# Half of the gate products moved into attention, with the recurrence on VectorE and softmax sums from a block of ones

## What is computed

```python
xn = rms_norm(x, g_mix_norm)
z = xn @ w_in
c_q, c_kv, k_r, u, gate_a, gate_b = jnp.split(z, IN_SPLITS, axis=-1)
q = (rms_norm(c_q, g_q_a) @ w_q_b).reshape(b, t, N_HEADS, QK_DIM)
...
attn = chunk_causal_mla(q_nope, q_rope, k_nope, kr_all, v, q_pos, k_pos)
u_c, lru_buf_new = causal_dwconv(u, lru_buf, lru_conv_w, lru_conv_b)
rec, h_last = rg_lru(u_c, h0, w_rg, b_rg, w_ig, b_ig, lru_lambda)
mixed = jax.nn.sigmoid(gate_a) * attn + jax.nn.sigmoid(gate_b) * rec
x = x + mixed @ w_out
up = rms_norm(x, g_ffn_norm) @ w_up
up_c, ffn_buf_new = causal_dwconv(up, ffn_buf, ffn_conv_w, ffn_conv_b)
gate, val = jnp.split(up_c, 2, axis=-1)
x = x + (jax.nn.silu(gate) * val) @ w_down
```

## Time and profile before

| | |
|---|---|
| median of 3 runs | 945.11 us (944.52 to 946.34) |
| the profiled execution | 945.21 us, span 943.3 us |
| mean granted TensorE clock | 0.982 of full speed |
| TensorE matmul busy | 899.4 us (95%), 6689 instructions |
| VectorE busy | 604.8 us (64%), 1182 instructions |
| ScalarE busy | 347.5 us (37%) |
| GpSimd busy | 238.3 us (25%) |
| chain that ended last | TensorE 86%, VectorE 6%, issue 4% |

### The profile page before, as it was taken

How to read it: one execution, slowest core, us unless ns; L and a number is a source line. 1 busy time by engine, 2 the same in 40 slices (tenths; PEclk the granted TensorE clock), 3 DMA queues, 4 the chain that set the end, 5 groups by cost and what they waited for, 6 DMA issues and landing times.

```text
span 943.3 us, 18508 instructions
## 1 busy us (share of the span) xinstructions
PE 899.4 (95%) x6689; PEld 847.8 (90%) x6689; DVE 604.8 (64%) x1182; ACT 347.5 (37%) x619; POOL 238.3 (25%) x278
## 2 busy tenths in 40 slices
PE   5999999998799999998999999999999999999998
PEld 5899999987577887776799999999999999999998
DVE  4378634686789888897544488777778777322221
ACT  6331455364344444442423533333333332112111
POOL 4000233462333221331012233333333333201000
PEclk8999999999899999997999999999999999999999
DMA  8333323322000000010003232233332222233321
GB/s 256 79 84 76 97 78 82 77 73 46 15 7 10 14 14 14 20 27 1 1 23 90 67 110 78 81 88 89 89 89 82 78 85 84 84 97 104 98 70 36
DMA packets 114630, 63.55 MB, mean 67 GB/s; under 512 B 7836, under 2 KB 113054, under 8 KB 114588
## 3 DMA queue, kind: packets, MB, share of 16 engines
q1 hardware_dynamic: 112396, 59.17, 22.4%
q0 software_dynamic: 2192, 3.81, 1.8%
HBM read 59.85 MB, written 2.70 MB: 66 GB/s over the span
## 4 chain that ended last, share of the span: by engine, by line
PE 86%; DVE 6%; issue 4%; ACT 2%; POOL 1%; SPq 1%; DMA 0%; DVEq 0%; ACTq 0%; POOLq 0%
PE PS L1141 61%; PE PS L1354 4%; PE PS L1338 4%; PE PS L1319 3%; PE PS L1176 3%; PE PS L1265 2%; PE PS L1308 2%; PE PS L1214 2%; PE PS L1261 1%; PE PS L1362 1%; PE PS L1292 1%; PE PS L1283 1%; DVE small L1010 1%; DVE w_lo L773 0%; PE PS L1325 0%
## 5 line engine op out<-in xcount | busy, mean ns | idle before, releaser
L541 ACT ACTIVATE w_hi<-w_raw 128x1024 fp32r<-128x1024 f32 (+2 forms) x104 | 107.6, 1035 | 368.7 <-PE PS L1141 354.4
L773 DVE TENSOR_TENSOR w_lo<-w_raw,w_hi 128x1024 fp32r<-128x1024 f32 (+2 forms) x104 | 128.1, 1231 | 122.8 <-ACT w_hi L541 122.6
L1141 PE MATMUL PS<-x2h,w_hi 128*128 128x274 f32 x704 | 147.7, 291 | 1.1 <-DVE w_lo L773 1.1
L1141 PE MATMUL PS<-x2h,w_lo 128*128 128x274 f32 x704 | 146.9, 290 | 0.0
L1141 PE MATMUL PS<-x2l,w_hi 128*128 128x274 f32 x704 | 146.9, 290 | 0.0
L1141 PEld LDWEIGHTS PS<-x2h,w_hi 128*128 128x128 f32 x704 | 111.9, 189 | 1.4 <-issue 1.3
L1141 PEld LDWEIGHTS PS<-x2l,w_hi 128*128 128x128 f32 x704 | 112.0, 189 | 0.0
L1141 PEld LDWEIGHTS PS<-x2h,w_lo 128*128 128x128 f32 x704 | 111.4, 189 | 0.0
L1141 PE MATMUL PS<-xnh,w_hi 128*128 128x274 f32 x384 | 83.3, 299 | 4.4 <-DVE w_lo L773 2.3
L1141 PE MATMUL PS<-xnl,w_hi 128*128 128x274 f32 x384 | 81.7, 295 | 0.0
L1141 PE MATMUL PS<-xnh,w_lo 128*128 128x274 f32 x384 | 81.0, 293 | 0.0
(11 more groups left out here) (254 smaller groups left out, 1706.6 us busy)
## 6 DMA issues: line engine op xcount, KB each, us to landing
w_raw<-in_w_up_dram SPq DMA_DIRECT2D x44, 512.0 KB, 3.8
w_raw<-in_w_in_dram SPq DMA_DIRECT2D x24, 512.0 KB, 3.9
w_raw<-in_w_down_dram SPq DMA_DIRECT2D x16, 512.0 KB, 3.7
w_raw<-in_w_out_dram SPq DMA_DIRECT2D x8, 512.0 KB, 4.1
w_raw<-in_w_down_dram SPq DMA_DIRECT2D x8, 384.0 KB, 3.9
xnat<-in_x_prompt_dram SPq DMA_DIRECT2D x4, 512.0 KB, 5.0
w_raw<-in_w_in_dram SPq DMA_DIRECT2D x4, 416.0 KB, 4.7
wq<-in_w_q_b_dram SPq DMA_DIRECT2D x8, 192.0 KB, 2.5
```

The source lines that it names most:

```text
L541: nc.scalar.activation(hi[:, slot % 2, 0:n], raw[:, slot % 4, 0:n], ACT.Copy).then_inc(s_hi, 1)
L773: tt(lo[:, slot % 2, 0:n], raw[:, slot % 4, 0:n], hi[:, slot % 2, 0:n].bitcast(F32), ALU.subtract).then_inc(s_lo, 1)
L1141: last = mm(PS[:, 2 * rank + j, 0:HT], w[:, slot % 2, cols], x[:, k0 + k, j * HT:(j + 1) * HT], start=(k0 + k == 0 and first), stop=(k0 + ...
```

## The change

Only twelve items stand ahead of attention (`FIRST`: A0, B0, U0 to U7, A1, B1). The other twelve gate items are computed inside attention, in halves of 24 matmuls (`gate_half`, banks 0 and 1), two items in pairs 0 to 4 and one in pairs 5 and 6 (`fills`). The sigmoids of the two branch gates become (1 + tanh(x/2))/2. The recurrence runs among the first products: squares of `a` go from GpSimd to ScalarE, the two products a block from GpSimd to VectorE. The key and query squares go from GpSimd to ScalarE. `V` gets a block of ones, so that a value matmul with a stationary tile of 128 columns leaves the sum of exponentials in the other 64 partitions; `values` now write banks 3 and 5, scores rotate over banks 2 and 4, and the transposition is a plain one with `ident`. ScalarE copies the sums (`head_sums`), VectorE takes their reciprocals over 128x274, twice a pair, one pair later (`sums_inverse`), and GpSimd multiplies and adds (`mix`). The first two output items are begun with k up to 6 and finished after that. `Kn` and `Qn` lie on the same memory as `th0` and `uc0` of the LRU's first four blocks. The hand-written loops up to attention are unrolled.

```diff
+FIRST = [("A", 0), ("B", 0)] + [("U", n) for n in range(KD)] + [("A", 1), ("B", 1)]
...
+I_LAT, I_IN = 0, 4
+I_G = I_IN + NF
+I_OUT = I_G + 12
...
+    return ("BA"[item % 2], 2 + (item - I_G) // 2)
...
+    return [I_G + 2 * p, I_G + 2 * p + 1] if p < 5 else [I_G + 5 + p] if p < 7 else []
...
+        zone = place
+        Kn = fixed("Kn", [P, 2, NKT, 2, NOPE])
...
+        th0 = fixed("th0", [P, 4, T])
+        uc0 = fixed("uc0", [P, 4, T])
...
-                                         accum_out=sm[:, 0:1]).then_inc(s_e, 1)
+                    nc.scalar.activation(Pn[:, n % 3, 0:w], bank[:, 0:w], ACT.Exp, bias=sm[:, 2:3]).then_inc(s_e, 1)
...
+                act.wait_ge(s_pv, 9 * p + 4 * (h + 1))
+                if h == 0 and p:
+                    act.wait_ge(s_mix, p)
+                nc.scalar.activation(sums[rows(h), 0:SEQ], values_bank(h)[rows(1 - h), :], ACT.Copy).then_inc(s_sum, 1)
...
             act.wait_ge(s_rec, 4)
...
+            for u in range(6):
+                evacuate_kq(0, u, (0, 1, 2, 3, 0, 1)[u])
+            squares_keys(0)
+            lru_gates(7)
+            squares_queries(0)
...
+                a_n = U[:, n, LEAD:]
+                dve.wait_ge(s_bt, n + 1)
+                step.on(nc.vector.tensor_copy(a_n[:, S0 - 1:S0], zero[:, 0:1]))
+                link(nc.vector.tensor_copy(uc(n)[:, S0 - 1:S0], vec[:, V_H0 + n:V_H0 + n + 1]))
+                nc.vector.tensor_tensor_scan(a_n, a_n, uc(n), 0.0, ALU.mult, ALU.add).then_inc(s_rec, 1)
...
+            def lru_input(n):
+                dve.wait_ge(s_mult, n + 1)
+                dve.wait_ge(s_iu, n + 1)
+                tt(uc(n), th(n), uc(n), ALU.mult).then_inc(s_bt, 1)
...
+                dve.wait_ge(s_lrui, n + 1)
+                tt(uc(n), tmp[:, n % 2, :], uc(n), ALU.mult).then_inc(s_iu, 1)
...
-            def row_inverse(p, n):
-                dve.wait_ge(s_e, p * 9 + (n + 1))
-                sm = small[:, 4 + n % 3, :]
-                if n < 8:
-                    link(nc.vector.reciprocal(sm[:, 1:2], sm[:, 0:1]))
...
+            def gate_half(item, j):
+                kind, m = gate_of(item)
+                if j == 0:
+                    dve.wait_ge(s_gp, item - I_G + 1)
...
-                ts(dg[:, n % 3, :], ident[:, :], sm[:, 1:2], None, ALU.mult).then_inc(s_dg, 1)
...
+                cols = slice(j * HT, (j + 1) * HT)
+                tt(gate(kind, m)[:, cols], PS[:, j, 0:HT], rsT[:, cols], ALU.mult).then_inc(s_gf, 1)
...
+            def gated_values(p, h):
+                g_p = gate("A", p)[rows(h), 0:SEQ]
+                dve.wait_ge(s_gt, gate_count("A", p))
+                dve.wait_ge(s_pv, 9 * p + 4 * (h + 1))
+                stt(g_p, g_p, 1.0, values_bank(h)[rows(h), :], ALU.add, ALU.mult).then_inc(s_o, 1)
...
+            def sums_inverse(p, j):
+                cols = slice(j * HT, (j + 1) * HT)
+                dve.wait_ge(s_sum, 2 * p + 2)
+                dve.wait_ge(s_o, 3 * p + 3)
+                ins = nc.vector.reciprocal(sums[:, cols], sums[:, cols])
+                if j:
+                    ins.then_inc(s_ri, 1)
...
+                    if n == 3:
+                        if following:
+                            columns(p + 1, 0, 0)
+                            columns(p + 1, 1, 1)
+                        if p:
+                            sums_inverse(p - 1, 0)
+                        if following:
+                            gate_half(gate_items[0], 0)
+                    if n == 4:
+                        gated_values(p, 0)
+                        if p:
+                            sums_inverse(p - 1, 1)
+                        if 1 <= p <= 5:
+                            split_item(17 + 2 * p)
+                        if following:
+                            gate_half(gate_items[0], 1)
...
+                        lru_m2(q)
+                if g == 8:
+                    for q in range(2):
+                        lru_input(q)
+                        recurrence(q)
+            evacuate_first(9)
+            gated_input(5)
+            conv(7)
+            for q in range(2, 4):
+                lru_input(q)
+                recurrence(q)
+            split_item(I_IN + 11)
+            gated_input(6)
...
+            def gate_half(item, j):
+                pe.wait_ge(s_lo, item + 1)
+                for k in range(KD):
+                    cols = slice(k * P, (k + 1) * P)
+                    for w, x, first in ((hi, xnh, True), (hi, xnl, False), (lo, xnh, False)):
+                        last = mm(PS[:, j, 0:HT], w[:, item % 2, cols], x[:, k, j * HT:(j + 1) * HT],
+                                  start=(k == 0 and first), stop=(k == KD - 1 and w is lo))
+                last.then_inc(s_used if j else s_gp, 1)
...
-                    last = mm(bank[:, a * P:(a + 1) * P], Pn[:, n % 3, a * P:(a + 1) * P], dg[:, n % 3, :], start=True, stop=True)
+                    last = nc.tensor.transpose(bank[:, a * P:(a + 1) * P], Pn[:, n % 3, a * P:(a + 1) * P], ident[:, :])
...
-                        last = mm(PS[h * VD:(h + 1) * VD, 3, t * P:(t + 1) * P], V[:, par, a, h, :], PT[:, b, a * P:(a + 1) * P],
...
+                        last = mm(values_bank(h)[:, t * P:(t + 1) * P], V[:, par, a, h:h + 2, :].rearrange("p h n -> p (h n)"),
...
+                    if following and n == 3:
+                        for v in range(2):
+                            if kq:
+                                pe.wait_ge(s_kqf, 6 * (p + 2) + 5 + v)
+                            else:
+                                pe.wait_ge(s_vf, 3 * p + 2 + v)
+                            transpose_kq(p + 1, v, v)
+                        pe.wait_ge(s_trf, 5 * (p + 1) + 1)
+                        gate_half(first, 0)
+                    if following and n == 4:
+                        pe.wait_ge(s_trf, 5 * (p + 1) + 2)
+                        gate_half(first, 1)
+                    if following and n == 5:
+                        for v in (2, 3):
...
+                    keys_queries(0, 0, 0)
+                    keys_queries(0, 1, 1)
+                    pe.wait_ge(s_free, 10)
+                    keys_queries(0, 2, 2)
+                    keys_queries(0, 3, 3)
+                    for u in (4, 5):
+                        pe.wait_ge(s_kqf, u - 3)
+                        keys_queries(0, u, u - 4)
+                    lru(7)
...
+            def output_product(r, k0, nk):
...
+            for r in range(2):
+                if r:
+                    pe.wait_ge(s_e, 9 * NP_)
+                    pe.wait_ge(s_o, 3 * NP_ - 2)
+                    pe.wait_ge(s_sum, 2 * NP_ - 1)
+                pe.wait_ge(s_lo, I_OUT + r + 1)
+                output_product(r, 0, KD - 1)
+            for r in range(2):
+                output_product(r, KD - 1, 1).then_inc(s_used, 1)
+            for r in range(2, KD):
                 pe.wait_ge(s_free, G_OUT + r - 1)
```

More of the change, by code:

```diff
@@ L369, in _ @@
+            for t in range(I_OUT + 6, I_UP):
+                w_out_item(t)
             with sp.Fori(0, NU // 4) as it:
@@ L715, in _ @@
+            act.wait_ge(s_free, 12)
+            gate_tanh(gate("B", 1))
+            for u in range(4, 6):
+                evacuate_kq(1, u, u - 4)
+            squares_keys(1)
+            last_states(1)
+            for u in range(3):
+                evacuate_v(0, u, (0, 1, 5)[u])
+            exps(0, 0)
+            squares_queries(1)
+            for p in range(NP_):
+                attend(p)
+            mixed_hi(7)
             with act.Fori(0, 2) as it:
@@ L1396, in _ @@
[L1396 to L1410 removed]
+                        scores(p + 1, n - 7)
+                    transpose_probs(p, n)
```

1087 lines of the change are left out of this document (627 added, 460 removed).

## The result

The changed kernel takes 915.62 us (median of 4 runs, 914.76 to 915.99) against 944.82 us of the kernel before on the same chip: a ratio of 0.969, 95% interval 0.9674 to 0.9706. It is 29 us faster, where 18 were forecast. The profiled execution has a span of 914.2 us.

What follows compares the result with a forecast made beforehand. The prediction took TensorE as the bound, with VectorE second. Its terms, start -3.7, first products +5.8, attention -24.0 and output +3.5, sum to -18.4 us: 927 us from a median of 945.11, range 911 to 940.

Steps and rivals of the forecast that it cites:

- rival 2: Better packing: start chains side by side (-12), attention stalls 4 us, sample loads hidden (-7); 905 to 918 us, chance 0.22.
- The start: Up to the first product: a 2.09 us wait and 1.6 us of lower clock go, -3.7 us.
- (b): First products, up to the second pair of scores: waits and low clock grow from 21.6 to 27.4 us, +5.8 us.
- The first wait: First products: evacuation of pair 0's keys waits for recurrences 0 to 3 on VectorE, 7.3 us of TensorE wait.
- With 7 us of small waits: First products: small waits besides the two large ones, put at a third of what there was.
- the second place: Before attention goes on: VectorE has 22 us queued after the last square of `a`, TensorE some 12; 10 us wait.
- The terms for transposes, sample records and the reciprocal: Attention: plain transposes save about 2.8 us a pair, sample records take 0.11 us each (+1.1 a pair), a reciprocal 1.9.
- In the groups of 128 moving columns that is free: Attention: value matmuls loading 128 stationary columns instead of 64 cost nothing extra in these groups.
- The gate halves stand where TensorE used to wait for maxima and exps, so I keep 1.5 ...: Attention: gate halves fill waits, so stalls fall from 20.7 to 9.0 us, part of the attention term of -24.0 us.
- Output: Output items: item 2 waits for a split behind item 0's evacuation, +3.5 us, bounds 0 and +4.5 with lower clock.
- Rival 4: Attention: VectorE binds at steps 3 and 4; reciprocals of 3.3 us each eat the gain, 957 us at 4; chance 0.08.
- Rival 5: Attention: gate halves don't replace stalls, since TensorE runs in order; 20 us of stalls, 938 to 940 us, chance 0.08.

Runs made afterwards that it cites:

- E10: Changed kernel with the four lru_input products ahead of recurrences 0 and 1, pair 0's key evacuation waiting for those products alone: 914.62 us.
- E9: Changed kernel with output item 1 begun with k up to 2 only, then item 0 finished, then the rest of item 1: 912.13 us.
- E1: Changed kernel with the prompt's value matmuls on stationary tiles of 64 columns again: 930.45 us.
- E4: Changed kernel with each gate half inside attention cut to its first slice of k, 3 of 24 matmuls: 901.14 us.
- E12: E6 with scores rotating over two banks in place of three and two reciprocals of 128x274 put into every pair: 924.48 us.
- E6: Kernel before with plain transposes waiting for the exponentials alone, no reciprocals, no `diag`, no normalisation, and 128-column value matmuls: 896.07 us.
- E3: Kernel before with the prompt's value matmuls on 128 columns, both heads at once, `diag` products kept: 946.28 us.
- E5: Kernel before with plain transposes by the identity; VectorE still forms `diag` and TensorE still waits for it: 946.01 us.
- E2: Changed kernel with the sample's value matmuls alone on stationary tiles of 64 columns: 911.50 us.
- E7: Changed kernel with each wide reciprocal of pairs 0 to 6 done twice: 946.56 us.

## Why the prediction was right, and where it was off

The time lies in the range, below the likeliest case's own of 918 to 936 us, and in the band of rival 2. The four terms are off by +1.2, -6.9, -6.8 and +1.7 us, 11 us in sum, and behind the third stand two larger errors of opposite sign. That the sum still came within 11 us is in part luck.

**The start** was right in its wait, 2.1 us. The 1.6 us of low clock were counted twice in the prediction: they lie behind the first product, so in the 202.9 us from which (b) starts.

**The first products.** The first wait was forecast to 0.4 us, by the queue that VectorE has on the trace too. "With 7 us of small waits" was mis-sized: 1.7 us of them were there (0.51 and 1.18), and the second place measured 7.5, not 10. So there are 16 us of waits and some 4 of low clock in place of the forecast 27.4 (whose terms add to 27.3). E10 shows that the first wait was real and not cover for the second: with 6.93 down to 1.63 us (and the 1.18 ahead of it up to 2.21) the second place stayed as it was, at 2.75, 0.89 and 2.10 us. Its fourth piece, 1.60 us, is not a cost of its own: it is 0.23 us in E10 and 0.20 in E9, which changes nothing there, and the time from the first piece's end to the fourth's is 11.0 us in all three, so the matmuls between take longer where it is short. That the recurrence moved to VectorE, and the squares to ScalarE, was not tried by itself.

**Attention.** The terms for transposes, sample records and the reciprocal each hold within 0.1 us. The step that failed is "In the groups of 128 moving columns that is free": it is a gain of 0.22 us a group, 14.8 us by E1, since tiles of one width only are left in the prompt's steps. The prediction read 0.122 us a record for value records too; its own timeline has 0.133 for them (0.80 for six). Against it, 9 us of stalls were forecast and 15.7 measured, 9.2 of them at one place, the gate half behind the columns of keys, for which the prediction had no term. Of the 20.7 us of stalls that it found in the kernel before, 13.6 are waits and the rest is lower clock (0.97 in pair 0, 0.84 in pair 6); in the changed kernel's attention the clock is 1.00 throughout.

"The gate halves stand where TensorE used to wait for maxima and exps, so I keep 1.5 ..." had the right sign for the wrong reason. The waits are not fewer; the gate halves cover costs that the block of ones creates (E4: 50 us, with the clock), and which outside come to 28 us (E12 against E6). With the gate items inside, the changed kernel is 20 us above E6, and 9 below E12. And a deeper assumption was not stated at all: that work taken from TensorE is time. In the kernel before it isn't (E3 and E5: 14 and 22 us of work for nothing). In the changed one, work added costs its full time (E1: 14 us of lengths, 14.8 of time), but of work taken out E2 keeps half and E4 less than a quarter.

**Output.** The wait of 3.46 us was forecast at 3.5; the 1.6 us of low clock behind it stood in the bounds and not in the term.

**The rivals.** Rival 2's range holds, but by none of its reasons: the two start chains don't run beside each other (E10), and what came less there were the small waits; attention's stalls were 15.7 and not 4 us; and the sample loads weren't hidden. Its hit is luck. Rival 4 was close: it was put at 3.3 us for a reciprocal, and E7 shows the whole gain gone at 3.7. Rival 5 has the sum of the waits right, 15.7 us where they were 13.6, but not their place: before, all were for `diag`, and now most are for the columns of keys. Its 938 to 940 us leaves out the clock and the value groups.

## What to carry to other kernels

Before work is taken from an engine, ask whether that engine or a chain across engines is the bound: shorten the work alone in the old kernel and see if the waits grow or the clock falls. Two edits that give nothing each may give 50 us with a third that takes a link out of the chain, and with it the work of the engine that held it. Independent work on the busiest engine, placed among the steps of such a chain, pays for costs on other engines; where a step waits once in every round, moving a few matmuls of the same step into the gap is worth trying, together with the other long waits rather than alone.
